# Norm statistics kept with tokens on partitions in a two-block transformer kernel

## The reference, cut to what matters

```python
def _rms_norm(h, g):
    hf = h.astype(jnp.float32)
    hf = hf * lax.rsqrt(jnp.mean(hf * hf, axis=-1, keepdims=True) + NORM_EPS)
    return (hf * g.astype(jnp.float32)).astype(h.dtype)

def layer_norm(x):
    xf = x.astype(jnp.float32)
    mu = jnp.mean(xf, axis=-1, keepdims=True)
    var = jnp.mean(jnp.square(xf - mu), axis=-1, keepdims=True)
    return ((xf - mu) * lax.rsqrt(var + LN_EPS)).astype(x.dtype)
```

## Time and profile before

| | us |
|---|---|
| median of 3 runs | 3102.87 |
| lowest and highest | 3100.55, 3104.77 |
| the profiled execution | 3104.1 |
| its span in the trace | 3102.3 |
| TensorE, matmuls busy | 2959.7 |
| VectorE busy | 1316.5 |
| ScalarE busy | 539.0 |

### The profile page before, as it was taken

How to read it: one execution, slowest core, us unless ns; L and a number is a source line. 1 busy time by engine, 2 the same in 40 slices (tenths; PEclk the granted TensorE clock), 3 DMA queues, 4 the chain that set the end, 5 groups by cost and what they waited for, 6 DMA issues and landing times.

```text
span 3102.3 us, 50418 instructions
## 1 busy us (share of the span) xinstructions
PE 2959.7 (95%) x21400; PEld 1945.2 (63%) x21400; DVE 1316.5 (42%) x3023; ACT 539.0 (17%) x1200; POOL 0.2 (0%) x4
## 2 busy tenths in 40 slices
PE   7999899999999999999999999999999889988998
PEld 5455699994444434557745555544568678867887
DVE  1467788876898977404321111111121432023211
ACT  2113333321211111204300000000011310022000
POOL 0000000000000000000000000000000000000000
PEclk8999999999999999999999999999999999999999
DMA  7232001004777875320289999999963235522551
GB/s 266 94 136 81 1 1 42 1 15 141 230 238 225 253 228 184 127 82 15 85 320 387 374 369 376 375 393 385 378 228 109 69 94 153 145 82 64 153 149 55
DMA packets 351330, 551.00 MB, mean 178 GB/s; under 512 B 14256, under 2 KB 292144, under 8 KB 347792
## 3 DMA queue, kind: packets, MB, share of 16 engines
q1 hardware_dynamic: 351120, 547.89, 50.6%
HBM read 546.80 MB, written 1.05 MB: 177 GB/s over the span
## 4 chain that ended last, share of the span: by engine, by line
PE 90%; DVE 5%; ACT 2%; DMA 2%; issue 1%; SPq 0%; DVEq 0%; ACTq 0%
PE bank L669 16%; PE bank L1336 15%; PE bank L1128 9%; PE bank L1352 7%; PE bank L1527 7%; PE bank L930 7%; PE bank L1142 4%; PE bank L634 3%; PE bank L748 3%; PE bank L1169 2%; PE bank L1073 2%; DVE mix L2083 2%; PE bank L914 1%; DMA arena<-in_ada_w 1%; PE bank L1203 1%; PE bank L1295 1%
## 5 line engine op out<-in xcount | busy, mean ns | idle before, releaser
L669 PE MATMUL bank<-a,ring 128*128 128x256 f32 (+1 forms) x1792 | 453.4, 415 | 15.4 <-ACT a L1624 8.3
L2083 DVE SCALAR_TENSOR_TENSOR mix<-arena,csil,mix 128x256 f32<-128x256 f32 x1008 | 402.2, 480 | 43.1 <-ACT mix L1628 43.0
L669 PEld LDWEIGHTS bank<-a,ring 128*128 128x128 f32 x1792 | 343.6, 193 | 121.9 <-issue 70.2
L1336 PE MATMUL bank<-ring,arena 128*32 128x352 f32 x5376 | 404.5, 461 | 4.9 <-DVE small L2642 4.9
L1336 PEld LDWEIGHTS bank<-ring,arena 128*32 128x32 f32 x5376 | 176.4, 110 | 227.9 <-issue 226.9
L1128 PE MATMUL bank<-a,ring 128*128 128x512 f32 x704 | 307.9, 597 | 6.8 <-ACT a L1624 6.8
L1128 PEld LDWEIGHTS bank<-a,ring 128*128 128x128 f32 x704 | 133.3, 191 | 180.0 <-issue 178.0
L1527 PE MATMUL bank<-arena,ring 128*128 128x256 f32 x1024 | 223.5, 379 | 2.0 <-DVE arena L2795 2.0
L1352 PE MATMUL bank<-ring,arena 128*32 128x256 f32 x3840 | 213.3, 379 | 0.0
L2678 DVE TENSOR_TENSOR arena<-arena,bank 128x352 f32<-128x352 f32 x48 | 25.0, 521 | 443.0 <-ACT arena L1892 443.0
L1527 PEld LDWEIGHTS bank<-arena,ring 128*128 128x128 f32 x1024 | 194.4, 190 | 29.1 <-DVE arena L2795 2.8
(11 more groups left out here) (414 smaller groups left out, 3181.2 us busy)
## 6 DMA issues: line engine op xcount, KB each, us to landing
ring<-in_moe_w SPq DMA_DIRECT2D x224, 704.0 KB, 9.2
ring<-in_moe_w SPq DMA_DIRECT2D x160, 512.0 KB, 6.6
ring<-in_mlp_w SPq DMA_DIRECT2D x64, 1024.0 KB, 5.5
arena<-in_ada_w SPq DMA_DIRECT2D x96, 512.0 KB, 4.1
arena<-in_w_ada SPq DMA_DIRECT2D x48, 512.0 KB, 3.6
ring<-in_ffn_w SPq DMA_DIRECT2D x22, 1024.0 KB, 8.7
arena<-in_moe_w SPq DMA_DIRECT2D x32, 704.0 KB, 10.3
h<-in_w_ada SPq DMA_DIRECT2D x8, 2048.0 KB, 7.5
```

Of the source, the lines that this page charges most:

```text
L669: i = mm(bank[b][:, 0:n], ws[:, k, t * P:t * P + P], rhs[:, k, sl], start=(k == 0), stop=(k == KT - 1))
L1336: i = mm(b[32 * t:32 * t + 32, 0:PART], ac_[:, g, 32 * k:32 * k + 32], by_tile(ws[i_], t), start=(k == 0), stop=(k == KT - 1), skip_group_ ...
L2083: ins = V.scalar_tensor_tensor(dst, x, cond, dst, ALU.mult, ALU.add)
```

## The change

Steps 2 to 4 are made with the tokens on the partitions. The squares become the stationary operand, 128 features by 128 tokens, and one column of `mean` the moving one, so that a block of 128 tokens gives one column of 128 sums: 4 columns for 512 tokens, 2 for 256. ScalarE takes the root from PSUM with epsilon as the bias, a column of a small tile set at the start; VectorE takes the reciprocal of the 2 or 4 columns. TensorE then multiplies the column, broadcast to 128x128 as the stationary operand, with the identity (`rstd_rows`), which puts the values along the free dimension in all 128 rows of the bank. VectorE multiplies the tiles by the bank. The sum of epsilon on VectorE is gone. `rstd_rows` waits for VectorE's reciprocal in TensorE's stream, directly behind the sums, except at stage 13 (two tiles later) and stage 3 (behind one small matmul). Stage 1 uses bank 5 for its sums instead of bank 0, and ScalarE takes the root of stage 13 one tile earlier.

```diff
--- before.py
+++ after.py
@@ -283,6 +283,8 @@
         mods = cut(sb("mods", 384), 0, 192, 2)
         gs = cut(sb("gs", 128), 0, 8, KT, 2)
         tmpA, tmpB = sb("tmpA", T), sb("tmpB", T)
+        stats = sb("stats", 12)
+        eps, std, rstd = stats[:, 0:2], stats[:, 4:8], stats[:, 8:12]
         small = sb("small", 800)
         arena = sb("arena", 15872)
         bank = [ctx.enter_context(nc.psum_tensor(f"bank{b}", [P, 512], F32))[:, :] for b in range(8)]
@@ -471,7 +473,7 @@
 
         CENTRED = {st: hT if st == 13 else aT for st in (5, 6, 7, 8, 9, 10, 11, 12, 13)}
         SQUARES = {st: aT if st in (0, 1, 2, 4) else mix for st in range(14)}
-        SUM_BANK = {st: {4: 4, 13: 3}.get(st, 0) for st in range(14)}
+        SUM_BANK = {st: {1: 5, 4: 4, 13: 3}.get(st, 0) for st in range(14)}
 
         block = ctx.enter_context(nc.Block())
 
@@ -638,11 +640,24 @@
             def square_in(st, sl, k):
 
                 pe.wait_ge(act_done, at(AC, ("square", st, k)))
-                add_tile("norm sum", st, k, SQUARES[st][:, k, sl], SUM_BANK[st])
+                for h in range((sl.stop - sl.start) // P):
+                    o = sl.start + P * h
+                    i = mm(bank[SUM_BANK[st]][:, h:h + 1], SQUARES[st][:, k, o:o + P], const("mean")[:, 0:1],
+                           start=(k + h == 0), stop=(k == KT - 1), skip_group_check=True)
+                if k == KT - 1:
+                    i.then_inc(pe_done, did(PE, ("norm sum", st)))
 
             def squares_in(st, sl):
                 for k in range(KT):
                     square_in(st, sl, k)
+
+            def rstd_rows(st, sl):
+
+                pe.wait_ge(vec_done, at(VE, ("rstd", st)))
+                for h in range((sl.stop - sl.start) // P):
+                    i = mm(bank[SUM_BANK[st]][:, P * h:P * h + P], rstd[:, h:h + 1].broadcast_to([P, P]), ident,
+                           start=True, stop=True, skip_group_check=True)
+                i.then_inc(pe_done, did(PE, ("rstd rows", st)))
 
             def mean_after(st, before_st):
 
@@ -706,6 +721,7 @@
 
             pe.wait_ge(consts_in, 16)
             squares_in(0, slice(0, T))
+            rstd_rows(0, slice(0, T))
             pe.wait_ge(vec_done, at(VE, "ada bank"))
             pe.wait_ge(act_done, at(AC, ("cond", 3)))
             for k in range(KT):
@@ -1090,6 +1106,7 @@
                 if j:
                     square_in(1, slice(0, T), j - 1)
             square_in(1, slice(0, T), KT - 1)
+            rstd_rows(1, slice(0, T))
 
 
             def sum_up(g):
@@ -1149,7 +1166,7 @@
             turn_later(FT + KT - 1)
             square_in(2, slice(0, T), KT - 1)
             turn_later(FT + KT)
-            pe.wait_ge(vec_done, at(VE, ("var", 2)))
+            rstd_rows(2, slice(0, T))
 
 
             product("q1", first["qkv"], 4, aT, LAT, [1, 2],
@@ -1235,6 +1252,8 @@
                 square_in(3, LAT, j)
                 if j == 1:
                     squares_in(13, CTX)
+                if j == 3:
+                    rstd_rows(13, CTX)
 
             product("na out", first["na_out"], 4, o1, slice(0, TL), [4, 5],
                     lambda j: pe.wait_ge(vec_done, at(VE, ("na res", j))), then=beside)
@@ -1242,7 +1261,7 @@
             counts.count[PEM] = per
             mm(bank[7][:, 0:8], const("ones"), const("count", 8), start=True, stop=True
                ).then_inc(pe_moe, per)
-
+            rstd_rows(3, LAT)
 
             pe.wait_ge(router_in, 16)
             ws = router_w
@@ -1385,6 +1404,7 @@
             pe.wait_ge(ve_moe, blocks * vper + vper)
             outputs_back().then_inc(pe_done, did(PE, "back last"))
             squares_in(4, LAT)
+            rstd_rows(4, LAT)
 
 
             def context_keys(j):
@@ -1412,6 +1432,7 @@
             mean_after(5, 4)
             context_keys(2)
             squares_in(5, LAT)
+            rstd_rows(5, LAT)
             context_keys(3)
             context_values(0)
             context_values(1)
@@ -1509,11 +1530,13 @@
                         lambda j: pe.wait_ge(vec_done, at(VE, (name, j))),
                         then=lambda j: residual_mean(name, st, j))
                 squares_in(st, LAT)
+                rstd_rows(st, LAT)
 
             def mlp(i, st):
 
                 mean_after(st, st - 1)
                 squares_in(st, LAT)
+                rstd_rows(st, LAT)
                 product(("mlp1", i), first["mlp1", i], 16, aT, LAT, [2, 3],
                         lambda j: pe.wait_ge(vec_done, at(VE, ("relu2", i, j))), of=st)
                 pe.wait_ge(vec_done, at(VE, ("relu2", i, F2T - 1)))
@@ -1531,6 +1554,7 @@
                         residual_mean(("mlp", i), st + 1, n - 1)
                 residual_mean(("mlp", i), st + 1, KT - 1)
                 squares_in(st + 1, LAT)
+                rstd_rows(st + 1, LAT)
 
             outwards("out2", first["out2"], 6, mix)
             mlp(0, 7)
@@ -1538,6 +1562,7 @@
 
             mean_after(9, 8)
             squares_in(9, LAT)
+            rstd_rows(9, LAT)
             n = 0
             for c in range(2):
                 for g in range(0, KT, 2):
@@ -1585,9 +1610,13 @@
 
             def root(st, sl):
 
-                n = sl.stop - sl.start
-                ac.wait_ge(vec_done, at(VE, ("var", st)))
-                act(tmpB[:, 0:n], tmpA[:, 0:n], ACT.Sqrt).then_inc(act_done, did(AC, ("sqrt", st)))
+                c = (sl.stop - sl.start) // P
+                e = int(st in CENTRED)
+                if st == 0:
+                    ac.wait_ge(vec_done, at(VE, "eps"))
+                ac.wait_ge(pe_done, at(PE, ("norm sum", st)))
+                act(std[:, 0:c], bank[SUM_BANK[st]][:, 0:c], ACT.Sqrt, bias=eps[:, e:e + 1]
+                    ).then_inc(act_done, did(AC, ("sqrt", st)))
 
             def centred_squares(st, sl):
 
@@ -1859,7 +1888,7 @@
                 ac.wait_ge(vec_done, at(VE, ("centre", 13, k)))
                 square(13, CTX, k)
             for k in range(KT):
-                if k == 4:
+                if k == 3:
                     root(13, CTX)
                 ac.wait_ge(vec_done, at(VE, ("na res", k)))
                 square(3, LAT, k)
@@ -1998,31 +2027,27 @@
                     V.tensor_tensor(CENTRED[st][:, k, sl], hT[:, k, sl], bank[2 if st == 13 else 1][:, 0:n],
                                     ALU.subtract).then_inc(vec_done, did(VE, ("centre", st, k)))
 
-            def variance(st, sl):
+            def inverted(st, sl):
+
+                c = (sl.stop - sl.start) // P
+                ve.wait_ge(act_done, at(AC, ("sqrt", st)))
+                V.reciprocal(rstd[:, 0:c], std[:, 0:c]).then_inc(vec_done, did(VE, ("rstd", st)))
+
+            def scaled(st, sl):
 
                 n = sl.stop - sl.start
-                ve.wait_ge(pe_done, at(PE, ("norm sum", st)))
-                V.tensor_scalar(tmpA[:, 0:n], bank[SUM_BANK[st]][:, 0:n],
-                                LN_EPS if st in CENTRED else RMS_EPS, None, ALU.add
-                                ).then_inc(vec_done, did(VE, ("var", st)))
-
-            def scaled(st, sl):
-
-                n = sl.stop - sl.start
-                ve.wait_ge(act_done, at(AC, ("sqrt", st)))
-                V.reciprocal(tmpA[:, 0:n], tmpB[:, 0:n]).then_inc(vec_done, did(VE, ("rstd", st)))
-                ve.wait_ge(vec_done, now(VE))
+                ve.wait_ge(pe_done, at(PE, ("rstd rows", st)))
                 src = CENTRED[st] if st in CENTRED else hT
                 dst = hT if st == 13 else aT
                 for k in range(KT):
-                    V.tensor_tensor(dst[:, k, sl], src[:, k, sl], tmpA[:, 0:n], ALU.mult
+                    V.tensor_tensor(dst[:, k, sl], src[:, k, sl], bank[SUM_BANK[st]][:, 0:n], ALU.mult
                                     ).then_inc(vec_done, did(VE, ("norm", st, k)))
 
             def norm(st, sl):
 
                 if st in CENTRED:
                     centre(st, sl)
-                variance(st, sl)
+                inverted(st, sl)
                 scaled(st, sl)
 
             def op(name, ins):
@@ -2038,6 +2063,8 @@
                                            ).then_inc(vec_done, did(VE, (name, j) if s else (name, j, "ctx")))
 
 
+            V.memset(eps[:, 0:1], RMS_EPS).then_inc(vec_done, did(VE, "eps 0"))
+            V.memset(eps[:, 1:2], LN_EPS).then_inc(vec_done, did(VE, "eps"))
             V.memset(bank[7], 0.0).then_inc(vec_done, did(VE, "ada bank"))
             for h in range(2):
                 V.memset(xpad[:, 4 * h:4 * h + 4, :, :], 0.0
@@ -2552,7 +2579,7 @@
                 ve.wait_ge(pe_done, at(PE, ("na out", j)))
                 residual("na res", j, bank[4 + j % 2][:, 0:TL], (0, 1, 2), (1,))
                 if j == 3:
-                    variance(13, CTX)
+                    inverted(13, CTX)
                 if j == 4:
                     scaled(13, CTX)
 
```

## The result

| | before | changed |
|---|---|---|
| median of 12 runs, us | 3102.59 | 3112.34 |
| lowest and highest | 3096.93, 3107.22 | 3110.67, 3124.63 |
| ratio, 95% interval | | 1.0045 (1.0034 to 1.0057) |
| profiled execution, its span | 3104.1, 3102.3 | 3110.67, 3108.9 |
| granted clock, mean over that span | 0.975 | 0.970 |

3112.0 was forecast.

What follows compares the result with a forecast made beforehand. TensorE is busy 95% of the span, mostly in untouched dense products, so gains come only where it waits for a norm. Place terms, 2.9 - 2.0 - 2.1 - 0.6 + 4.2 + 3.9 + 2.4 + 0.4 = +9.1, give 3112.0 us; range 3094 to 3124.

Steps and rivals of the forecast that it cites:

- rows 6: Profile rows where 64 16-column matmuls without idle time drop the clock to 0.50; so narrow sums lose it, 1.7 to 3.0 us each.
- Sums at equal clock: New sums, one moving column per load: +0.12 us per 256-token norm, +0.29 per 512-token norm.
- Chain: Last sum to first scaling: 1.3 us at full clock, 1.65 at half, instead of 2.7; with 512 tokens 1.75 instead of 4.8.
- Stage 0: First norm: narrow sums stay at half clock to 24.7, modulation products end at 36.2; +3.8 less 0.9, so +2.9 us.
- Stage 1: 512-token norm: shorter chain and sums -2.8, clock fall closer to the following product +0.8, so -2.0 us.
- Stages 13 and 3: Extra TensorE work under the output product +0.7, shorter chain of stage 3 -1.3; together -0.6 us.
- Stages 4 and 5: Keys and values wait behind the sums for the statistics, then run at fallen clock: +4.2 and +3.9 us.
- Stages 6 to 11: Three pairs: chains and sums -2.6 each, lost clock +3.4 each; +0.8 per pair, +2.4 us in all.
- A: Rival: the clock stays where it is today, sum -11.5, 3091.4 us; chance 0.18.
- B: Rival: clock lost only in stages 0, 4 and 5, pairs -1.0 each; +2.3, 3105.2 us; chance 0.24.
- C: Rival: clock loss lasts twice as long at stages 0, 4, 5 and one per pair; about +20, 3123 us; chance 0.10.
- D: Rival: PSUM-source root takes 0.42 or more and scaling 0.3 more, 13 norms x 0.5; 3118 us; chance 0.06.

Runs made afterwards that it cites:

- E1: Changed kernel with 128 moving columns instead of one in each pass of the sums; 3083.59 us, ratio 0.9938.
- E2: Kernel before with only the sums of stages 6 to 12 in the new narrow layout, old chain kept; 3107.7 us, ratio 1.0016.
- E8: E1 with one moving column at stages 6 to 12; 3100.20 us, ratio 1.0001.
- E12: E5 measured again on one chip beside E11; 3078.59 us, ratio 0.9924.
- the trace of the second group: Changed kernel run again without edit, its slowest run profiled; median 3115.28 us, runs 3109.96 to 3123.4.
- E9: E1 with the roots spread and VectorE taking the wide reciprocal of the bank, as before the change; 3107.06 us, ratio 1.0019.
- E3: Changed kernel with 128 moving columns in the sums of stage 0 alone; 3118.34 us.
- E4: Changed kernel with the spreading matmuls of stage 4 behind the first context key product, those of stage 5 behind the last; 3118.07 us.
- E5: E1 with spreading matmuls of stages 4 and 5 behind context key products, ScalarE's epsilon wait moved before stage 0's squares; 3078.81 us, ratio 0.9931.
- E11: E1 measured again on one chip beside E12; 3083.92 us, ratio 0.9941.

## Why the prediction was right, point by point

The time, the sign and the range were right, and the step that carried them, rows 6, is what E1, E2 and E8 showed: narrow matmuls without idle time do not hold the clock. The size was in part luck. The two traces are 6.6 apart, the medians 9.75 and the means 13.4, and the forecast of 9.1 was worked out for a trace; by places, its misses cancelled. Nor did every run of sums lose the clock, as was counted: in the first trace stages 4, 5, 7 and 11 keep 1.00 within them.

- **Sums at equal clock**: 32 passes 3.73 against 3.72, forecast +0.12 per 256-token norm. Next to nothing, as forecast.
- **Chain**: 1.30 at the full clock as forecast; 1.81 at half, forecast 1.65 (the four passes are 1.24 there). With 512 tokens 1.76 in E1, forecast 1.75.
- **Stage 0**: sums end at 24.92 (24.7), the modulation is applied 3.8 later (39.28 against 35.47), forecast +2.9. The step that was missing is the table load: ScalarE now has two waits before its root, and the load of 1.28 runs behind the second one instead of under the sums. E12, with one wait there, has it at 14.79 again.
- **Stage 1**: from the last sum of stage 1 (771.35 and 775.15, 3.8 apart) to the scaling the offset falls by 2.1. The forecast had -2.8 for this, at the full clock, and +0.8 for the clock in the product behind; the eight passes ran at half, and the product lost 1.7. So -0.4, forecast -2.0: the clock term was mis-sized. Another 1.7 are lost near 1175, where a stretch at half clock lasts longer in the same products, and no term of the sum has them. In E1 the offset grows by 1.5 over the same products, in the changed kernel by 3.4; more was not tried. **Stage 2**: from 5.1 to 2.8, -2.3, forecast -2.1.
- **Stages 13 and 3**: forecast -0.6, measured +0.8 (offset 1.95 before the output product, 2.77 at the router). The mis-sized term is the sums of stage 13: 36 narrow passes in a row inside a product. I priced them at 0.1 as they had no wait beside them; the product tile behind them took 5.39 instead of 3.62.
- **Stages 4 and 5**: forecast +8.1, measured +5.9 (offset 3.05 at the last sum of stage 4, 8.95 where the values of the context begin). Waits and rows were +2.0 and +1.7, forecast 1.6 (1.5 by its own figures, 2309.2 less 2307.67) and 1.3. The clock was over-sized: 0.9 and 1.2 in the dense keys, forecast 2.5 each.
- **Between the places**: 0.9 come back near 1432 and 1.8 near 2436 (offset 8.95 to 7.1), where the kernel before has a stretch at half clock and the changed one has none. No term has them either.
- **Stages 6 to 11**: forecast +2.4, measured -0.2 in the first trace (7.1 to 6.9), and 6.2 more in the trace of the second group (4.3 to 10.5 behind the first; the sums of stage 12 add 2.2). I gave one number for a term that has two.
- **Stage 12**: forecast +0.4, measured -0.3.

The rivals. A, the clock held, was rightly unlikely, but its size was wrong. I took the kernel before as the state with the clock held and put the sum at 3091.4; E1 holds it from stage 7 on and gives 3083.6, because in the kernel before the clock fell in the long waits too. The step that failed there is "the clock stays where it is today": a shorter wait is worth its length and the clock that the longer one loses (E9). The means at the full clock take 4.14, not the 3.7 that I took, so the dearest fall (6.68) costs 2.5 and not 3.0. B, that the clock lost in the pairs costs little, is near the first group in the pairs, though not in the total (3105.2), C's size (3123) the second. D is out: root 0.26, no dearer scaling (2.73 for 8 tiles).

The sentence of the Trainium skill that was weighed ("TensorE: Matmul & The Clock Gate", "What's actually happening", the gate goes by how busy the PE has been recently) agrees with the traces only if busy isn't read as "has an instruction under way". PE is shown busy for 6.86 of 6.90 us in the sums of stage 10 of the changed kernel, at a granted 0.51, and for 3.80 of 3.80 in those of stage 8 of E1, at 1.00.

## What to carry to other kernels

Price a matmul by its pitch and by its width apart. A matmul bound by its weight load could have 128 moving columns for nearly nothing here (32 passes 3.84 against 3.73), and those idle columns, written to bank space that nobody reads, were worth 28 us. Before a total is read as a loss, put the trace beside one of the same group: E3 and E4 had their gains all along. A chain shortened on VectorE also pays in TensorE's clock, but a wait that is put in TensorE's own stream should have independent products in front of it, and a second wait before a ScalarE instruction can push its table load behind the wait.

## What the runs showed of the hardware that I had not expected

- Padding the sums from 1 to 128 columns took 3112 to 3084 us although 32 passes went from 3.73 to 3.84.
- One kernel can have two times 12 us apart (3110 to 3112.5, 3122 to 3125), with identical instructions, as half-clock stretches cover different parts of it. The spread is 2 and 4 us in E5 and E12, but 7 in E1 and E11, whose sums are as wide.
- ACT_TABLE_LOAD (1.28) was issued ahead of a single wait (14.51 at stage 0 before) and behind the last of two (25.00 after).
